# Order of the six matmuls of a weight tile: one token half after the other, in a split-precision encoder step

## What is computed

```python
def swiglu(x, w1, w2):
    g, u = jnp.split(x @ w1, 2, axis=-1)
    return (jax.nn.silu(g) * u) @ w2

for l in range(DEPTH):                       # 2 layers
    h += 0.5 * gate1 * rmsnorm(swiglu(mod1(rmsnorm(h)), w1, w2))
    x = mod2(rmsnorm(h)); p = x @ w_in       # q, k, v of two attentions, u and v of a gating MLP, gate logits
    m = sig(gA) * (oA @ W_a) + sig(gB) * (oB @ W_b) + sig(gC) * (oC @ W_c)
    h += gate2 * rmsnorm(m @ w_out)
    h += 0.5 * gate3 * rmsnorm(swiglu(mod3(rmsnorm(h)), w1b, w2b))
```

## Time and profile before

| what | value |
|---|---|
| median of 3 runs | 2849.2 us (2848.51 to 2849.84) |
| the profiled execution, its own time | 2847.8 us |
| its span in the profile | 2846.0 us |
| granted TensorE clock, mean | 0.997 |
| TensorE matmul busy | 2783.9 us, 98% of the span |
| TensorE weight load busy | 2628.9 us, 92% |
| VectorE busy | 1298.3 us, 46% |
| ScalarE busy | 971.0 us, 34% |
| GpSimd busy | 111.2 us, 4% |

### The profile page before, as it was taken

The page is one execution under the profiler, slowest core; times in us unless marked ns, Lnnn a source line. Parts: engine busy times, 40 slices in busy tenths (PEclk is TensorE's granted clock), DMA queues, the critical chain, the costliest instruction groups (busy, mean ns, idle before and its releaser), DMA issues.

```text
span 2846.0 us, 49978 instructions
## 1 busy us (share of the span) xinstructions
PE 2783.9 (98%) x21654; PEld 2628.9 (92%) x21654; DVE 1298.3 (46%) x2533; ACT 971.0 (34%) x1821; POOL 111.2 (4%) x210
## 2 busy tenths in 40 slices
PE   7999999999999999999999999999999999999997
PEld 6999999878999989999999999998889999999997
DVE  3444424655544464443264443256555445544423
ACT  4222324444422452222252222244443225422322
POOL 0000000010000000000000000001100000000000
PEclk9999999999999999999999999999999999999999
DMA  6444532333222234432224444323322222222221
GB/s 245 149 148 149 172 121 93 110 123 98 92 82 82 82 104 149 148 134 88 88 86 152 149 149 165 112 100 116 122 96 68 82 82 75 82 82 82 86 87 66
DMA packets 90186, 319.82 MB, mean 112 GB/s; under 512 B 11360, under 2 KB 14464, under 8 KB 89776
## 3 DMA queue, kind: packets, MB, share of 16 engines
q1 hardware_dynamic: 64048, 222.50, 23.4%
q0 software_dynamic: 25920, 94.14, 9.7%
HBM read 305.70 MB, written 11.55 MB: 111 GB/s over the span
## 4 chain that ended last, share of the span: by engine, by line
PE 85%; DVE 7%; ACT 3%; DVEq 2%; issue 2%; DMA 1%; SPq 0%; ACTq 0%
PE ps L668 77%; PE ps L782 2%; PE ps L1013 2%; PE ps L1059 1%; DVE h L1671 1%; ACT w_hi L1162 1%; DVE x_lo L1678 1%; PE ps L1035 1%; DVEq L1670 1%; DVE z L1669 1%; PE ps L677 1%; DMA w_raw<-in_f 1%; ACT sig L1498 1%; ACT x_hi L1254 1%; DVEq L2017 1%
## 5 line engine op out<-in xcount | busy, mean ns | idle before, releaser
L668 PE MATMUL ps<-x_hi,w_hi 128*128 128x290 f32 (+1 forms) x4256 | 973.8, 304 | 22.7 <-DVE x_lo L1678 13.6
L668 PE MATMUL ps<-x_lo,w_hi 128*128 128x290 f32 (+1 forms) x4256 | 935.4, 295 | 0.0
L668 PE MATMUL ps<-x_hi,w_lo 128*128 128x290 f32 (+1 forms) x4256 | 934.8, 295 | 0.0
L668 PEld LDWEIGHTS ps<-x_hi,w_hi 128*128 128x128 f32 x4256 | 686.7, 189 | 95.1 <-issue 65.3
L668 PEld LDWEIGHTS ps<-x_lo,w_hi 128*128 128x128 f32 x4256 | 701.1, 190 | 0.3
L668 PEld LDWEIGHTS ps<-x_hi,w_lo 128*128 128x128 f32 x4256 | 692.7, 189 | 0.0
L1553 DVE TENSOR_TENSOR w_lo<-w_raw,w_hi 128x1024 fp32r<-128x1024 f32 x386 | 468.8, 1222 | 254.2 <-ACT w_hi L1162 251.9
L1162 ACT CAST w_hi<-w_raw 128x1024 fp32r<-128x1024 f32 x386 | 392.9, 1047 | 77.3 <-DMA w_raw<-in_f 77.3
L668 PE MATMUL ps<-hid_hi,w_hi 128*128 128x288 f32 x1344 | 300.8, 295 | 1.8 <-DVE c_col L1610 1.8
L668 PE MATMUL ps<-hid_hi,w_lo 128*128 128x288 f32 x1344 | 300.7, 295 | 0.0
L668 PE MATMUL ps<-hid_lo,w_hi 128*128 128x288 f32 x1344 | 298.7, 293 | 0.0
(11 more groups left out here) (214 smaller groups left out, 2391.8 us busy)
## 6 DMA issues: line engine op xcount, KB each, us to landing
w_raw<-in_f SPq DMA_DIRECT2D x260, 512.0 KB, 3.5
ada_w<-in_ada POOLq DMA_DIRECT2D x128, 512.0 KB, 5.7
w_raw<-in_gate SPq DMA_DIRECT2D x64, 512.0 KB, 3.5
w_raw<-in_tri SPq DMA_DIRECT2D x42, 512.0 KB, 3.5
ada_first<-in_ada SPq DMA_DIRECT2D x4, 2048.0 KB, 17.7
w_raw<-in_wout SPq DMA_DIRECT2D x16, 512.0 KB, 3.4
decay_s<-f_scratch POOLq DMA_DIRECT2D x16, 272.0 KB, 6.0
decay_p<-f_scratch POOLq DMA_DIRECT2D x8, 512.0 KB, 5.9
```

The costliest lines, as they stand in the source:

```text
L668: r = mm(ps[:, 2 * out + b, 0:width], w, xx[:, cols(b)], start=first and n == 0, stop=last and n == 2)
```

## The change

Within a weight tile the loop over the halves is now the outer one and the loop over the three products the inner one. In tiles of odd number within their chunk, half 1 comes first; the middle product is no longer reversed. Calls with one half are as they were. After the edit `split_tile`'s matmuls carry line 667.

```diff
             s = c % SLOTS
             wh, wl = w_hi[:, s, t * P:(t + 1) * P], w_lo[:, s, t * P:(t + 1) * P]
-            for n, (w, xx) in enumerate(((wh, hi), (wh, lo), (wl, hi))):
-
-                for b in halves[::-1] if cols is columns and n == 1 else halves:
-                    width = cols(b).stop - cols(b).start
+            for b in halves[::-1] if t % 2 else halves:
+                width = cols(b).stop - cols(b).start
+                for n, (w, xx) in enumerate(((wh, hi), (wh, lo), (wl, hi))):
                     r = mm(ps[:, 2 * out + b, 0:width], w, xx[:, cols(b)],
                            start=first and n == 0, stop=last and n == 2)
             return r
```

## The result

| | before | after |
|---|---|---|
| median of 5 runs | 2848.75 us (2848.38 to 2849.84) | 2860.55 us (2860.04 to 2861.45) |
| profiled execution | 2847.8 us | 2860.9 us |
| span | 2846.0 us | 2859.1 us |

The change makes the kernel slower by 11.8 us: ratio 1.0041, 95% interval 1.0027 to 1.0056. The forecast was 5.2 us slower, 2854.4, with a range of 2841 to 2867.

The account below looks back on a forecast made before the run. TensorE's matmul pace was taken to bound the kernel. Terms of 4.2 us (288/288 columns) and 1.0 us (288/290), the rest zero, made 5.2 us slower: 2854.4 us on the median, range 2841 to 2867.

Parts of the forecast that it names:

- the price per distance: On 288/288 columns, matmul start-to-start 132.5 ns within a half, 131.25 across; on 288/290, 133.4 within, 133.3 across.
- What bounds the kernel: Whole kernel: TensorE's matmuls, busy 98% of the span; only their pace can move, 1 ns on each of 16680 is 16.7 us.
- Weight loads, banks, the end of a chunk cost zero: Changed tiles: repeated weight load 190 ns, new one 189; chunk end still waits for the pair; 0 us.
- The halves alone keep their paces: Calls with one half, 1656 matmuls: unchanged, `hid` stretches at 133.2 and 131.8 ns; 0 us.
- The term on 288/288: 4776 matmuls: 4020 slower by 0.63 ns and 756 by 2.3 ns, all to 132.3; 4.2 us slower.
- the 130.0 beat: Six of 28 output tiles on `hid`, 756 matmuls at 130.0 ns, were to go to 132.3; 1.7 us slower.
- The term on 288/290: 11904 matmuls on `x`: five of six distances at 133.4 ns, the mean of both halves, against 133.3; 1.0 us slower.
- The premise under both: Each tile's pace splits into distances within a half and across: two and four before on 288/288, five and one after.
- Order is free: Rival: the instruction alone sets the distance, differences come from addresses and entry; time stays 2849.2 us; chance 0.1.
- the slower rival: On `x` the wide half sets the whole tile's beat, 134.6 ns; 17.1 us slower, 2866.3; chance 0.2.
- The faster rival: Staying on a half brings `x` toward 132.2 ns; 10.9 us gained against 4.2 lost, 2842.5 us; chance 0.15.
- The counts that would show it wrong: 220 us window on `x`: over 1663 matmuls (under 132.3 ns) or under 1637 (over 134.4) refutes the prediction.

Follow-up runs that it names:

- s2_banks: Seven patterns separating token half, PSUM bank and weight tile, run where a kernel tried seven matmul orders; grouped banks 133.3 ns per matmul, w_hi for w_lo 132.8.
- The seven orders: One kernel running seven orders of a tile's six matmuls, each on its own chunks and output tiles; 131.7 to 134.2 ns per matmul on `hid`.
- p_moving: Kernel before with the change's order on `x` alone (288/290 columns), the rest as before; 2856.21 us, ratio 1.0024.
- p_flip_x: Kernel before with halves on `x` going 010101 in even tiles, 101010 in odd; `hid`, `o`, `m` as before; 2842.70 us, ratio 0.9976.

## Why the prediction was right, and where its size was wrong

The time was forecast to rise, within 2841 to 2867 us, and it did. It rose by 11.8 us where 5.2 had been forecast, and the price per distance behind the 5.2 did not hold. What bounds the kernel was read rightly; that the sign came out as forecast is in part luck.

- *What bounds the kernel.* Right. Waits, clock and the count of instructions are as before, and the pace of TensorE's matmuls is all that moved.
- *Weight loads, banks, the end of a chunk cost zero.* `s2_banks` shows it for the alternation of the weight tiles and for the banks. The end of a chunk no run takes by itself; the waits after it are as before. The reading of the earlier trace rows was weak support: the 4256 loads with 189 ns are those of `w_lo`, of which every second repeats the tile just loaded.
- *The halves alone keep their paces.* Right, 133.2 and 131.6 ns.
- *The term on 288/288.* Forecast 4.2 us, measured 5.4 alone. The pace was to be 132.3 and is 132.7; that the 130.0 beat would go too was right.
- *The term on 288/290.* Forecast 1.0 us, measured 7.2 alone, about 6.4 of it on `x`. This is the step that was mis-sized: "I take the mean, because both halves are issued equally often". By that mean the order would take 133.4; it takes 133.8 to 134.0. The two ends of this term, 132.2 and 134.6, did bound it.
- *The premise under both.* "I split the pace into distances within a half and distances across halves." That failed. On `hid` the order with all six distances across takes 133.3, not 131.25. The halves alone differ because they lie at two places against the weights, and a mixed sequence settles at a pace of its own: 134.2 for one, above both halves alone, 131.7 for another, that of the faster. The agreement on 288/288, 132.3 against 132.7, is chance to that extent. The prediction had named this way out: "the pace hangs on something longer than a pair of matmuls".
- *The rivals.* "Order is free" said that the differences come from addresses and entry. They do come from addresses, but through them the order counts; it is free only with both halves at one place. The measured time lies about midway between the forecast and the slower rival. That one had the right side and, at 17.1 us, the wrong mechanism: the pace on `x` did not go to the wide half's 134.6, and with equal widths the change costs more there, not less. The faster rival fell with the pace going up instead of down.
- *The counts that would show it wrong.* 1663 and 1637 matmuls in the window are 132.5 and 134.6 ns once the two that had begun before it are left out, and not 132.3 and 134.4. The measured 1646 lies between them either way.
- *The Trainium skill's rule.* The Trainium skill (TensorE: Matmul & The Clock Gate, Back-to-back issue gap) gives columns / 2.4 + 2.5 ns for a warm matmul, one distance per width, an estimate of 122.5 ns for 288 columns. It calls that the gap of a single matmul in isolation and says that in a stream of weight loads and matmuls both set the spacing; the prediction left this out. The seven orders of the same 288-column matmuls spread from 131.7 to 134.2 ns, so the trace does not agree with one distance per width. The same page (Step-by-step: what each phase is for) says that loading the next tile's weights takes no read bandwidth from the running matmul. Moving the weights by 128 bytes exchanged the paces of the two halves, 1.6 ns apart; here the measurement decides, and where the weights lie does reach the matmuls' pace. By what path, no run shows.

## What to carry to other kernels

Where TensorE is the bound and each matmul brings its own weight load, read the pace as start-to-start distance over a long stretch, and compare it between stretches of the same width: a difference of one nanosecond was 16.7 us here. Before choosing an order of the moving operands, look at where they start against the weights modulo 256 bytes; with 288 fp32r columns and both halves at the weights' residue, seven orders all took 131.7 ns. A pace measured in one pattern is no price for a mixed one: run the mixture, several to a kernel, each on its own tiles.

## What the runs showed of the hardware that was not expected

- In a row of matmuls with 288 fp32r columns whose moving operands all start at the weight tile's residue modulo 256 bytes, one costs 131.7 ns; where all start 128 bytes off, 133.3, whichever of the two arrays is moved, and whichever bank is written.
- Sequences of the two places take 130.0, 131.7, 132.8, 133.3 or 134.2 ns; the same sequence can hold two of these, and a change elsewhere can move it from one to the other: six output tiles at 130.0 before, two in `p_moving` and `p_flip_x`, with their own orders unchanged. What picks the beat, and what lies behind the beats, was not found. Only shifts of 128 bytes against each other were tried.
- Two more columns in one half of two add 1.1 ns to the mean matmul in the old order on `x` and 0.6 in the new.
